# Masked bias rows and contiguous bias tables: built in the two odd projection stages, or in the even attention

## What is computed

```python
rpb_cols = rpb[:, :, col_idx - cc[:, None] + NA_COLS - 1]      # 8 heads, 15 row offsets, 31 column offsets
def row_block(args):
    qr, ridx, ri = args
    bias = jnp.transpose(rpb_cols[:, ridx - ri + NA_MAX_ROWS - 1], (0, 2, 1, 3))
    s_loc = jnp.einsum('bchd,bicjhd->bhcij', qr, kr) * scale + bias
    ...
```

## Time and profile before

| what | us |
|---|---|
| median of 3 runs | 3068.68 (3063.66 to 3072.29) |
| the profiled execution's own time | 3067.87 |
| its span in the trace | 3066.1 |
| PE busy in the span | 2389.5 (78%) |
| DVE, ACT, POOL busy | 1566.4, 986.1, 610.4 |
| `attend_even` | 550, of which PE busy 471 |
| `project_tiles` | 205, of which PE busy 118 |
| `project_heads`, up to 2105 | 239, of which PE busy 212, DVE 202 |

### The profile page before, as it was taken

The page is one execution under the profiler, slowest core; times in us unless marked ns, Lnnn a source line. Parts: engine busy times, 40 slices in busy tenths (PEclk is TensorE's granted clock), DMA queues, the critical chain, the costliest instruction groups (busy, mean ns, idle before and its releaser), DMA issues. The chain is left out here.

```text
span 3066.1 us, 31465 instructions
## 1 busy us (share of the span) xinstructions
PE 2389.5 (78%) x10535; PEld 1758.6 (57%) x10536; DVE 1566.4 (51%) x2093; ACT 986.1 (32%) x1305; POOL 610.4 (20%) x599
## 2 busy tenths in 40 slices
PE   5499888899882799999922765995997836999980
PEld 0378655565650588888700554773665735888770
DVE  2255563443423555656444335994773235576754
ACT  1122243334220545545301211112653104455540
POOL 0133302111113100000012654220312321000002
PEclk9999989899995799999955887997998967999995
DMA  9211045312118667766287664665762245687936
GB/s 386 89 42 42 32 152 209 110 32 62 39 41 246 223 222 278 281 240 224 110 347 275 210 196 136 164 182 165 200 172 80 103 176 189 237 304 278 350 137 233
DMA packets 325628, 551.32 MB, mean 180 GB/s; under 512 B 124189, under 2 KB 168715, under 8 KB 319372
## 3 DMA queue, kind: packets, MB, share of 16 engines
q1 hardware_dynamic: 210976, 401.70, 38.3%
q0 software_dynamic: 26032, 85.59, 8.1%
q10 hardware_dynamic: 88508, 62.61, 6.5%
HBM read 438.00 MB, written 126.51 MB: 184 GB/s over the span
## 5 line engine op out<-in xcount | busy, mean ns | idle before, releaser
L2629 DVE TENSOR_TENSOR ex_gu_lo<-mw_gu,ex_gu_hi 128x2048 fp32r<-128x2048 f32 x128 | 287.3, 2287 | 77.8 <-ACT ex_gu_hi L2549 77.7
L2549 ACT ACTIVATE ex_gu_hi<-mw_gu 128x2048 fp32r<-128x2048 f32 x128 | 237.5, 1911 | 121.6 <-DVE ex_y L2676 115.7
L1659 PE MATMUL at_ps_o<-at_pT,at_v_one 128*128 128x512 f32 x336 | 178.6, 613 | 9.5 <-ACT at_total L1439 9.4
L2524 POOL TENSOR_TENSOR ex_at<-ex_slots,ex_nil 128x1 int32<-128x1 int32 x53 | 16.4, 309 | 805.6 <-PE ex_ps_x L2701 800.6
L2707 PE MATMUL ex_ps_g<-ex_gu_hi,ex_xT_hi 128*128 128x512 f32 x408 | 170.0, 417 | 8.2 <-issue 5.2
L2707 PE MATMUL ex_ps_y<-ex_d_hi,ex_hT_hi 128*128 128x512 f32 x408 | 166.7, 408 | 9.4 <-DVE ex_d_lo L2629 8.0
L2629 DVE TENSOR_TENSOR ex_d_lo<-mw_d,ex_d_hi 128x2048 fp32r<-128x2048 f32 x64 | 143.8, 2288 | 53.8 <-ACT ex_d_hi L2549 53.8
L1429 ACT ACTIVATE at_pT<-at_ps_s 128x512 f32<-128x512 f32 x168 | 99.7, 595 | 211.8 <-PE at_ps_s L1652 211.7
L2707 PE MATMUL ex_ps_g<-ex_gu_lo,ex_xT_hi 128*128 128x512 f32 x408 | 165.0, 404 | 0.0
L2707 PE MATMUL ex_ps_g<-ex_gu_hi,ex_xT_lo 128*128 128x512 f32 x408 | 164.7, 404 | 0.0
L2707 PE MATMUL ex_ps_y<-ex_d_hi,ex_hT_lo 128*128 128x512 f32 x408 | 162.0, 397 | 0.0
(11 more groups left out here) (465 smaller groups left out, 5759.3 us busy)
## 6 DMA issues: line engine op xcount, KB each, us to landing
mw_gu<-in_moe_w_gate SPq DMA_DIRECT2D x32, 2048.0 KB, 10.8
mw_gu<-in_moe_w_up SPq DMA_DIRECT2D x32, 2048.0 KB, 15.7
mw_d<-in_moe_w_down SPq DMA_DIRECT2D x32, 2048.0 KB, 7.8
y_d<-ex_y ACTq DMA_DIRECT2D x51, 512.0 KB
mod_mod_w<-in_ada_w SPq DMA_DIRECT2D x24, 1024.0 KB, 11.0
y_d<-at_zero POOLq DMA_DIRECT2D x36, 512.0 KB, 4.9
co_mod_w<-in_ada_w SPq DMA_DIRECT2D x16, 1024.0 KB, 13.8
edge_d<-rows_d ACTq DMA_DIRECT2D x64, 160.0 KB, 3.8
```

The lines of the kernel that those rows point to most:

```text
L1659: nc.tensor.matmul(ps_o[:, :], v_one[:, kt, g:g + 2, :].rearrange("p a d -> p (a d)"), pT[u % 3][:, :], start=(u == plan.first[i, g]), sto ...
L2524: nc.gpsimd.tensor_tensor(at[:, :], slots[:, bass.ds(within(n, most), 1)], nil[:, :], ALU.add).then_inc(S["at_ready"], 1)
L2549: nc.scalar.activation(dst, src, ACT.Copy).then_inc(sem, 1)
L2629: sub = lambda dst, a, b, sem: nc.vector.tensor_tensor(dst, a, as_f32(b), ALU.subtract).then_inc(sem, 1)
```

## The change

The masks and the copies leave `project_tiles` and `project_heads` and are put into `attend_even`, in a new class `BiasRows`. The instructions are the same in number and size. POOL's part: `begin` (two small clears, two loads of bias rows, two mask loads) ahead of the list of events, then one masked part at every even `values` from 0 to 62. The two loads of bias rows move from SP's queue to POOL's. ACT's part: one copy at each `scores` event from u = 40 to 135, right behind that step's exponential. The waits for the tables at the end of `project_heads` go, and ACT waits for them at the end of `attend_even`.

```diff
 project_tiles
-                sp.wait_ge(R["zero"], 2)
-                for i in range(2):
-                    sp.dma_start(bias_rows[i][:, P // 2 - 16:P // 2 + 15], rpbs[i].rearrange("h r c -> (h r) c")).then_inc(R["bias_in"], 16)
...
-                    if i == 5:
-                        for p in range(2):
-                            act.wait_ge(R[f"out{p}"], 16 * NP // 2)
-                    if 5 <= i < 9:
-                        o.copy_tables(act, k, 5 * (i - 5), 5 * (i - 4))
...
-                    if i < LT:
-                        for n in range(NP * i // 4, NP * (i + 1) // 4):
-                            mask_rows(n)
-                for p in range(2):
-                    pool.wait_ge(R[f"out{p}"], 16 * NP)
...
 project_heads
-                sp.wait_ge(o.tables_out, 16 * 96)
...
-                    o.copy_tables(act, k, 20 + 9 * j, 29 + 9 * j)
...
+class BiasRows:
...
+    def load_skew(self, pool, n):
+        i, part = divmod(n, self.NP)
+        pool.dma_start(self.skew[n % 2][:, :, :].rearrange("p c x -> p (c x)"),
+                       self.skews[i, part * self.PART * P:(part + 1) * self.PART * P].partition_broadcast(8 * 15)
+                       ).then_inc(self.skew_in[n % 2], 16)
+
+    def begin(self, pool):
+        for i in range(2):
+            self.nc.gpsimd.memset(self.bias[i][:, :], 0.0).then_inc(self.zeroed, 1)
+        pool.wait_ge(self.zeroed, 2)
+        for i in range(2):
+            pool.dma_start(self.bias[i][:, P // 2 - 16:P // 2 + 15], self.rpbs[i].rearrange("h r c -> (h r) c")).then_inc(self.bias_in, 16)
+        for n in range(2):
+            self.load_skew(pool, n)
+
+    def mask(self, pool, n):
+        i, part = divmod(n, self.NP)
+        if n == 0:
+            pool.wait_ge(self.bias_in, 32)
+        pool.wait_ge(self.skew_in[n % 2], 16 * (n // 2 + 1))
+        if n >= 2:
+            pool.wait_ge(self.out[n % 2], 16 * (n // 2))
+        self.nc.gpsimd.tensor_tensor(self.rows[n % 2][:, :, :], self.skew[n % 2][:, :, :], bc(self.bias[i][:, :], 1, self.PART), ALU.add
+                                     ).then_inc(self.made, 1)
+        pool.wait_ge(self.made, n + 1)
+        pool.dma_start(self.k.rows_d[i].rearrange("h r c x -> (h r) c x")[:, part * self.PART:(part + 1) * self.PART, :],
+                       self.rows[n % 2][:, :, :]).then_inc(self.out[n % 2], 16)
+        if n + 2 < 2 * self.NP:
+            self.load_skew(pool, n + 2)
...
+    def copy(self, eng, n):
+        o, m = divmod(n, 48)
+        if m == 0:
+            for p in range(2):
+                eng.wait_ge(self.out[p], 16 * self.NP // 2 * (o + 1))
+        dst, src = self.tables(o)[m]
+        eng.dma_start(dst, src).then_inc(self.copied, 16)
...
 attend_even, scalar
                         nc.scalar.activation(pT[u % 3][:, :], ps_s[u % 3][:, :], ACT.Exp).then_inc(S["exp_done"], 1)
                         if 2 <= u < 18:
                             split_w(u - 2, u - 1)
+                        if 40 <= u < 136:
+                            bias_rows.copy(act, u - 40)
...
+                bias_rows.finish(act)
 attend_even, gpsimd
                 pool.wait_ge(S["zero_ready"], 1)
+                bias_rows.begin(pool)
...
                     if what == 'values' and i >= 20 and zeroed < max_blocks(NT):
                         pool.dma_start(k.y_d[zeroed * P:(zeroed + 1) * P, :], zero[:, :]).then_inc(S["zeroed"], 16)
                         zeroed += 1
+                    if what == 'values' and i % 2 == 0 and masked < 2 * bias_rows.NP:
+                        bias_rows.mask(pool, masked)
+                        masked += 1
```

More of the change, by code:

```diff
@@ L706, in __init__, with project_tiles @@
         self.cols = ph.sb("cols", [P, 3, self.CC])
[L707 to L728, removed]
+def project_tiles(nc, k, w, o, dw, dw_b, ln_g, ln_b):
     CC = o.CC
@@ L742, in project_tiles @@
         ns.tile_used = S["gemm_g"]
[L743 to L748, removed]
         with nc.Block() as block:
@@ L1297, in event, with __init__, place, tables @@
         self.events.append((what, *a))
-def attend_even(nc, k, w_out):
+class BiasRows:
+    PART = 4
+    NP = GRID_W // PART
+    def __init__(self, rpbs, skews):
+        self.rpbs, self.skews = rpbs, skews
+    def place(self, ph, k):
+        self.nc, self.k = ph.nc, k
+        self.bias = [ph.sb(f"bias_rows{i}", [8 * 15, P]) for i in range(2)]
+        self.skew = [ph.sb(f"skew{i}", [8 * 15, self.PART, P]) for i in range(2)]
+        self.rows = [ph.sb(f"rows{i}", [8 * 15, self.PART, P]) for i in range(2)]
+        self.zeroed, self.bias_in, self.made = ph.sem("rows_zeroed"), ph.sem("rows_bias_in"), ph.sem("rows_made")
+        self.copied = ph.sem("rows_copied")
+        self.skew_in = [ph.sem(f"rows_skew_in{p}") for p in range(2)]
+        self.out = [ph.sem(f"rows_out{p}") for p in range(2)]
+    def load_skew(self, pool, n):
[25 more added lines that the diff above has]
+            self.load_skew(pool, n + 2)
+    def tables(self, o):
+        out, k = [], self.k
+        for h in range(8):
+            for half in range(2):
+                s = slice(half * GRID_W, (half + 1) * GRID_W)
+                for dst, r0, n in ((k.inner_d[o, h, s, :], (3, 4)[o], 8), (k.edge_d[o, h, s, 0, :], (5, 1)[o] - half, 10),
+                                   (k.edge_d[o, h, s, 1, :], (1, 5)[o] - half, 10)):
+                    src = bass.AP(k.rows_d.tensor, ((o * 8 + h) * 15 + r0) * GRID_W * P + P // 2 - 1,
+                                  [[P - 1, GRID_W], [GRID_W * P, n], [1, GRID_W]])
+                    out.append((dst.rearrange("p (s c) -> p s c", s=n), src))
+        return out
+    def copy(self, eng, n):
[5 more added lines that the diff above has]
+        eng.dma_start(dst, src).then_inc(self.copied, 16)
+    def finish(self, eng):
+        eng.wait_ge(self.copied, 16 * 96)
@@ L1303, in attend_even @@
+def attend_even(nc, k, w_out, bias_rows):
     plan = EvenPlan()
@@ L1328, in attend_even @@
         lT = ph.sb("lT", [NE, P])
+        bias_rows.place(ph, k)
         ps_s = [ph.ps(f"ps_s{i}", [P, 512]) for i in range(3)]
@@ L1476, in _ @@
                 pool.wait_ge(S["zero_ready"], 1)
-                zeroed = 0
+                bias_rows.begin(pool)
+                zeroed = masked = 0
                 for ev in plan.events:
@@ L2939, in build @@
                 return k
-            attend_even(nc, k, t['ev_w_out'][0])
+            attend_even(nc, k, t['ev_w_out'][0], BiasRows((t['c_rpb'][0], t['k_rpb_back'][0]), t['k_skew']))
         if stop == 'at0':
```

25 lines of the change are left out of this document (1 added, 24 removed).

## The result

The changed kernel takes 3089.74 us (median of 4 runs, 3086.07 to 3092.57), the kernel before 3066.58 beside it; the ratio is 1.0075, 95% interval 1.0063 to 1.0087. It is 23 us slower. I had forecast 3066.8 with a range of 3053 to 3081. The profiled execution has a span of 3088.6 us against 3066.1, at the same mean clock (0.886 and 0.887).

A forecast was written before the change was run, and what follows sets the result against it. It took `project_tiles` as bound by a chain through ACT, POOL and DVE, and `attend_even` by PE at many small waits. 3067.87 less 18.4 plus 17.3 gave 3066.8 us, range 3053 to 3081.

The forecast's parts named there:

- (c): `attend_even`, first tile: masked parts on POOL slow DVE's rests of the output weight; +5.5 us, bounds 0 and 12.
- (g): `attend_even`, later tiles: query loads land late beside the copies, 0.8 in each of three tiles; +2.5 us, bounds 0 and 8.
- (d): `attend_even`: zero writes and masked parts make POOL's root 2.6 late in two tiles; +2 us, bounds 0 and 6.
- (e): `attend_even`: PE's query loads under zero writes, with masked parts and copies added; +2 us, bounds -9 and +10.
- (a): `project_tiles`: `pc_x` of tiles 1 to 8 falls from 1.75 to 0.75, saving 8.0 us, plus 1.1 in the third.
- (b): `project_tiles`: without copies on ACT, `pc_hi` starts sooner after `cv_yT`, saving 9.3 us.
- (f): `attend_even`: copy issues on ACT delay drains (2.6) and the rest of `mixed` (2.7); +5.3 us, bounds 1 and 14.
- DMA backlog: Rival, chance 0.18: `attend_even` query loads come after a backlog of zero writes, masks and copies; 3081 us.
- The growth of `attend_even`: Sign: the stage grows from 550 by 12 to 22 us; prediction wrong if under 8 or over 27.

The follow-up runs named there:

- e1_masks_only: Changed kernel with the 96 copies back in their old places in the two odd stages, masks still in `attend_even`: 3086.60 us, ratio 1.0064 to the kernel before.
- e10_before_copies_heads: Kernel before with its 20 copies of `project_tiles` issued in `project_heads` as well: 3061.41 us, ratio 0.9981 to the kernel before.
- e3_masks_late: Changed kernel with copies at steps 72 to 167 and masked parts at even steps 24 to 86, none in the first tile: 3065.59 us, ratio 0.9988.
- e12_even_spread: Changed kernel with copies in `project_heads`, masked parts and zero writes alternating, each at every fourth step over the even stage: 3065.21 us, ratio 0.9994 to before.
- e14_after_norm: Changed kernel with copies in `project_heads`, five masked parts and five zero writes directly behind the norm in seven full tiles: 3065.75 us, ratio 0.9989 to before.
- e2_copies_late: Changed kernel with its copies at steps 72 to 167 instead of 40 to 135, behind the last zero write: 3076.03 us, ratio 1.0021 to before.
- e13_before_norm: Changed kernel with copies in `project_heads`, five masked parts and five zero writes between normal and mean in seven full tiles: 3038.97 us, ratio 0.9895 to before.

## Why the prediction was wrong

The gain in `project_tiles` was right; the terms (c) to (g) were summed at 17.3 and measured at 40.6, of which 14.4 are (c)'s place, 2.0 are (d)'s, some 24 are (e)'s place and 0.3 the later tiles. What failed is the price of the moved transfers: none in (c), a netted and too small one in (e), and none for an issue that stands.

- **(a) and (b), `project_tiles`: right.** -18.4 summed and measured. All ten `pc_x` take 0.75 now, against the earlier trace rows:

```profile
L312 DVE TENSOR_SCALAR pc_x<-pc_x,pc_rstd x10: 752/754/754, 1711.0 to 1875.9; 128x1024 f32<-128x1024 f32 x10
```

  The parts by themselves hold: 8.4 came with the masks gone (e1_masks_only, sum 9.1), 10.1 with the copies gone (e10_before_copies_heads, sum 9.3). That the total agrees to the tenth is luck: the two errors cancel.
- **`project_heads`: right.** 0.5 longer, where 0 was said with bounds of 0 and 3 shorter; the stage differs by more from one trace to the next.
- **(c), first tile: right in sign, wrong in cause.** 5.5 said, bounds to 12; 14.4 measured. I priced the adds that meet DVE's rests. The step that failed is that the parts' transfers got no price here: the weight pieces come one by one through two buffers, so ACT's waits for them doubled, 11.7 to 25.8. With the adds alone the second tile begins 3.1 later than in e3_masks_late, with the transfers alone 10.1. The rule cited from the Trainium skill (SBUF — State Buffer, "Who interferes with whom") is borne out by single rests of 1.36 and 1.67 us, and it carries 2 or 3 of the 14 us. The working was sound for what it priced, and the upper bound of 12 was passed because of what it left out.
- **(d), roots late: right.** POOL and PE after, third tile in order:

```profile
561.49 1.28 POOL L1510 TENSOR_TENSOR at_x<-at_x,at_tmp 128x512 f32<-128x512 f32 x1 [1.23 <-DVE at_tmp L1587]
...
570.32 0.59 POOL L1515 TENSOR_TENSOR at_rstd<-at_ms,mhalf 128x1 f32<-128x1 f32 x1
...
574.72 1.09 PE L1704 MATMUL at_ps_t<-ident,at_h 128*128 128x128 f32 x8 [1.81 <-POOL at_h L1518]
```

  From the addition's end to the root it is 7.55 us (7.4 said), PE waits 1.81 for h there and 0.23 a tile earlier: 2.0, as said.
- **(e), query loads under the zero writes: the main miss.** +2 said, +10 as its upper bound. The first wait went from 9.44 to 18.27, and at the next tile 16.6 us came, of which 1.8 are (d)'s: some 24 in all. Two steps failed. The first is the netting of the backlog: I had counted that parts "spread these writes out, which helps", and put their DMA time at 1 to 6 us. In the trace they don't spread them: POOL has time between its side events, and the parts come on top. The 1 to 6 was also short by its own rows: at the 354 GB/s of the earlier trace rows five parts of 480 KB are 6.9 us, and three parts with six copies of 0.70 are 8.4. The wait for a mask that was to throttle POOL took 3.8 us of the 30 from 504 on; for 19.1 POOL added or issued, with the DMA engines at 0.99. The second step is that (e) had a price only for loads that land late, none for an issue that stands. (f) bounded ACT's falling behind at 14 for the whole stage, and its forecast took 0.67 for each issue. ACT's 11.34 and 7.69 us, between which a single exponential starts, made most of the 16.6. The longest issue of a copy in the trace of before was 2.06 us, but SP's queue had shown the sign at the same two places, where its pair of query loads took 4.39 and 3.37 us to issue, against 1.24 to 1.33 elsewhere:

```profile
494.34 4.39 SPq L1366 DMA_DIRECT2D at_q_in_sb<-q_d  x2
...
552.19 3.37 SPq L1366 DMA_DIRECT2D at_q_in_sb<-q_d  x2
...
596.32 1.24 SPq L1366 DMA_DIRECT2D at_q_in_sb<-q_d  x2
```
- **(f), drains and `mixed` later: no cost.** 5.3 said; PE waits 0.69 for the drain at 728.88, against 0.68 in the earlier trace rows, and 1.36 for the rest of `mixed` at 656.39 and 708.06, as before. The step that failed is the 0.67 for an issue: I took it from five issues in a row with nothing beside them. Behind an exponential the issue runs beside that same exponential.
- **(g), query loads beside copies: near zero in the changed kernel** (the marks above leave 0.3 us for the late tiles, 2.5 said). The later kernels show 1.8 to 6.2 us at some of them once zero writes stand there too.
- **The rivals.** DMA backlog was right in mechanism and place (L1639 is its line now), and its point of decision, a first wait over 12, was passed. It was given 0.18 and a price of 31.5 for the stage, against 40.6 measured. It kept (c)'s 5.5 for the first tile, without the transfers; it did let ACT's issues stretch, at 8 in (f), and put 6 on the later tiles, where nothing came. That POOL "throttles itself" was my reason against it. In e12_even_spread and e14_after_norm POOL waits for its masks in the same way, and the met query loads still cost some 4 us each.
- **The growth of `attend_even`** is 40.6; over 27 the prediction was to be called wrong, and it is.

What stays open: why the same wait is 11.6 us in one execution and 22.1 in another; how the adds' 7 us by the times and 3 by the trace fit together; from which occupancy an issue on ACT stands, and whether SP's and ACT's issues, which overlap there, also held each other up. A masked part without its transfers through the first tiles of the changed kernel itself wasn't tried.

## What to carry to other kernels

When work with transfers is moved into another stage, look first for the loads on which that stage's critical engine waits, and for when they are issued; a burst that meets them costs far more than its share of the average bandwidth (a share raised from 0.15 to 0.35 cost nothing; with 0.91 instead of 0.46 in one 14 us window PE worked 5 us less). A slot in a list of steps is a place in time only for engines that wait in that step: tie the moved work to an event that its engine does wait for, and choose one that lies well before or after the sensitive load. Price an issue on a compute queue by what runs beside it, and where the DMA engines may be full, reckon with an issue that stalls everything behind it on its engine (11.34 and 7.69 us here).

## What the runs showed of the hardware

- An issue of a DMA on ACT's queue ran beside the activation in front of it (0.54 within 0.60), and the last 72 issues held nothing up. With the DMA engines at 0.98 two issues took 11.34 and 7.69 us, and SP's pair of query loads 7.44 to issue, 2.41 a tile earlier. In the kernel before that pair took 4.39 and 3.37 beside the zero writes and 1.24 to 1.33 elsewhere.
- The Trainium skill (DMA: Bandwidth & Descriptors, "Issuing engines are not separate DMA queues") says that DMAs of all issuers share 16 engines. The trace agrees in a stronger way than I had used it: zero writes and masks of POOL's queue made both SP's loads and ACT's issues late.
- Copies from DRAM to DRAM in pieces of 256 bytes, 73 of them in 270 us, more than doubled the DMA share (0.15 to 0.35) and left PE's 1005 matmuls in the same 270 us.
- Where the engines were full, executions of one kernel spread over 21 us (e2_copies_late, 3068.6 to 3089.6 in 10 runs); the kernel before over 12 in the 28 runs beside it (3061.2 to 3073.5), and e13_before_norm over 7 in 4 (3035.6 to 3042.4). The numbers of runs differ, so the last comparison is a hint only.
